# When the dots of the late rows are taken: fourth part instead of first, with their sends and one tile's transposes moved

## What is computed

```
s1, s2 = q . keys1, q . keys2            # 8 heads, 128 keys in each half
top 16 of each half, top 16 of their 256 sums -> eidx (of 16384 experts), gate = softmax
u = take(u_tab, eidx);  a = einsum('nhkd,nd->nhk', u, x)
w = gelu(a) * gate
y = einsum('nhk,nhkd->nd', w, take(v_tab, eidx))
```

## Time and profile before

| | us |
|---|---|
| median of 3 runs | 1452.32 (1451.91 to 1454.31) |
| profiled execution | 1451.67 |
| its span, first to last instruction | 1450.0 |
| PE busy | 1424.9 (98%) |
| PEld busy | 1266.6 (87%) |
| DVE busy | 1044.5 (72%) |
| POOL busy | 1017.7 (70%) |
| ACT busy | 608.9 (42%) |

### The profile page before, as it was taken

How to read it: one execution, slowest core, us unless ns; L and a number is a source line. 1 busy time by engine, 2 the same in 40 slices (tenths; PEclk the granted TensorE clock), 3 DMA queues, 4 the chain that set the end, 5 groups by cost and what they waited for, 6 DMA issues and landing times.

```text
span 1450.0 us, 24867 instructions
## 1 busy us (share of the span) xinstructions
PE 1424.9 (98%) x8029; PEld 1266.6 (87%) x8029; DVE 1044.5 (72%) x2204; ACT 608.9 (42%) x1018; POOL 1017.7 (70%) x631
## 2 busy tenths in 40 slices
PE   9999999999999999999999999999999999999996
PEld 5888788889999999999999999888888888888885
DVE  5466666688999989999987694875555555555587
ACT  5666741334333354444444443333333333333333
POOL 3332321335598877888877689898888888888886
PEclk9999999999999999999999999999999999999998
DMA  6212120424599889999999799999999999999981
GB/s 240 74 59 103 65 82 7 151 75 130 173 349 327 296 272 339 384 406 415 395 366 382 312 401 393 350 400 361 353 362 358 357 351 345 346 357 346 362 325 58
DMA packets 136907, 406.96 MB, mean 281 GB/s; under 512 B 13904, under 2 KB 56656, under 8 KB 134672
## 3 DMA queue, kind: packets, MB, share of 16 engines
q1 hardware_dynamic: 97088, 263.48, 50.3%
q0 software_dynamic: 39760, 142.76, 25.2%
HBM read 355.50 MB, written 50.14 MB: 280 GB/s over the span
## 4 chain that ended last, share of the span: by engine, by line
PE 85%; DVE 6%; ACT 2%; issue 2%; POOL 2%; DMA 2%; POOLq 0%; SPq 0%; ACTq 0%; DVEq 0%
PE banks L1824 14%; PE banks L1826 14%; PE banks L1825 14%; PE banks L1879 12%; PE banks L1881 12%; PE banks L1880 12%; PE banks L1941 2%; DMA raw<-u_t 1%; PE banks L2096 1%; PE banks L2097 1%; DVE rows L1363 1%; POOL lo L453 1%; PE banks L2033 1%; PE banks L1925 1%; DVE gate_hi L1593 1%
## 5 line engine op out<-in xcount | busy, mean ns | idle before, releaser
L453 POOL TENSOR_TENSOR lo<-raw,hi 128x1024 fp32r<-128x1024 f32 x292 | 706.8, 2422 | 349.5 <-ACT hi L447 330.2
L1824 PE MATMUL banks<-x1T_hi,hi 128*128 128x368 f32 (+3 forms) x1168 | 395.3, 338 | 0.7 <-POOL lo L453 0.4
L1825 PE MATMUL banks<-x1T_lo,hi 128*128 128x368 f32 (+3 forms) x1168 | 390.0, 334 | 0.0
L1826 PE MATMUL banks<-x1T_hi,lo 128*128 128x368 f32 (+3 forms) x1168 | 389.9, 334 | 0.0
L447 ACT ACTIVATE hi<-raw 128x1024 fp32r<-128x1024 f32 x292 | 307.1, 1052 | 30.2 <-DMA raw<-u_t 20.7
L1879 PE MATMUL banks<-hi,wgt_hi 128*128 128x512 f32 x750 | 291.8, 389 | 0.2 <-DVE wgt_lo L1701 0.2
L1881 PE MATMUL banks<-hi,wgt_lo 128*128 128x512 f32 x750 | 291.8, 389 | 0.0
L1880 PE MATMUL banks<-lo,wgt_hi 128*128 128x512 f32 x750 | 291.8, 389 | 0.0
L1701 DVE TENSOR_TENSOR wgt_lo<-wgt,wgt_hi 128x384 fp32r<-128x384 f32 x125 | 91.7, 734 | 193.0 <-ACT wgt_hi L1116 192.9
L1824 PEld LDWEIGHTS banks<-x1T_hi,hi 128*128 128x128 f32 x1168 | 219.3, 188 | 5.1 <-DVE x1T_lo L1335 0.6
L1826 PEld LDWEIGHTS banks<-x1T_hi,lo 128*128 128x128 f32 x1168 | 219.2, 188 | 4.4
(11 more groups left out here) (231 smaller groups left out, 1754.8 us busy)
## 6 DMA issues: line engine op xcount, KB each, us to landing
raw<-u_t SPq DMA_DIRECT2D x128, 512.0 KB, 5.6
raw<-v_tab SPq DMA_DIRECT2D x128, 512.0 KB, 6.8
g_scratch<-stage SPq DMA_DIRECT2D x12, 2048.0 KB, 11.0
gelu_scratch<-gelu SPq DMA_DIRECT2D x116, 192.0 KB, 7.5
ga<-gelu_scratch SPq DMA_DIRECT2D x29, 768.0 KB, 6.4
gg<-g_scratch SPq DMA_DIRECT2D x14, 1536.0 KB, 11.7
raw<-w SPq DMA_DIRECT2D x26, 512.0 KB, 3.4
raw<-w_pq SPq DMA_DIRECT2D x16, 512.0 KB, 3.5
```

Of the source, the lines that this page charges most:

```text
L453: eng.tensor_tensor(l[:, :], raw[:, c % RAW_SLOTS, :], h[:, :].bitcast(F32), ALU.subtract).then_inc(lo_ready, 1)
L1824: pe.matmul(o, h[:, s], hiT[:, k, tokens], start=(k == 0), stop=False)
L1825: pe.matmul(o, h[:, s], loT[:, k, tokens], start=False, stop=False)
L1826: ins = pe.matmul(o, l[:, s], hiT[:, k, tokens], start=False, stop=(k == KT - 1))
```

## The change

Eight edits, in the order of the program's time:

1. The six fill blocks of the last pair become twelve half blocks of three matmuls, at steps 2 to 7, 9 and 11 to 15.
2. x of the late tokens is no longer moved ahead of the search but in the first part (t = 7), into `sel[:, 0:2]`, free by then; `late_x` is no tensor of its own any more.
3. Four more gathers are asked for ahead of the first part (36 instead of 32); the gaps at tiles 25, 30 and 35 are filled, and tile 32 has two.
4. `turn_chosen` moves from tile 45 to tile 44, and `take_turned` stands ahead of tile 44's gelu.
5. In the first part GpSimd asks for 16 gathers (FIRST_MID_ROWS), all for the first 128 tokens, instead of 20, the first 16 of them for the late tokens.
6. The late numbers are moved at t = 2 of the first part (before: ahead of it, after tile 41), the late gates at t = 4 (before t = 3).
7. The late tokens' gathers and dots belong to the fourth part (LATE_O = 3). ScalarE puts their x into place near the end of the third part and takes it away near the end of the fourth; their weights are computed at the start of the fifth and moved at its t = 6 (before: after the second part).
8. So that the parts can differ, GpSimd's, VectorE's and some of ScalarE's and SyncE's loops over parts are written out.

```diff
-FIRST_ROWS_AT = (13, 13, 14, 15, 15, 16, 17, 17, 18, 19, 19, *range(20, 25), *range(26, 30),
-                 *range(31, 35), *range(36, 44))
+FIRST_ROWS_AT = (13, 13, 14, 15, 15, 16, 17, 17, 18, 19, 19, *range(20, 33), *range(32, 44))
 MID_ROWS = (2, 1, 1) * (MID_TILES // 3)
-LATE_ROWS = (0, 0, 0, 2, 3, 3, 2, 2, 2, 2, 2, 2)
+FIRST_MID_ROWS = (0, 0, 1, 1, 2, 2, 2, 2, 2, 2, 1, 1)
+LATE_O = 3
+R_LATE_AT = R_PRE + 2 * LATE_O
...
-        FILL_AT = {3: 0, 5: 1, 7: 2, 9: 3, 11: 4, 13: 5}
+        FILL_AT = (2, 3, 4, 5, 6, 7, 9, 11, 12, 13, 14, 15)
...
-            for g in range(SPREAD):
-                sp.dma_start(late_x[late_group(g), :], x1[LATE_AT:, TB - 1, :]).then_inc(late_x_moved, 16)
...
+            def move_x():
+                sp.wait_ge(sel_turned, 2)
+                for g in range(SPREAD):
+                    sp.dma_start(late_x[late_group(g), :], x1[LATE_AT:, TB - 1, :]).then_inc(late_x_moved, 16)
...
+            two_chunks(0, {2: move_numbers, 4: move_gates, 7: move_x})
+            with sp.Fori(1, LATE_O + 1) as o:
+                two_chunks(o)
+            two_chunks(LATE_O + 1, {6: move_weights})
...
+            for o in range(O_MID):
+                some_rows((R_PRE + 2 * o) * ROWS + AHEAD, 0, S_U + A_PRE + MID_TILES * o, 0,
+                          FIRST_MID_ROWS if o == 0 else MID_ROWS)
...
+            def late_dots_next():
+                act.wait_ge(late_x_moved, 16 * SPREAD)
+                act.wait_ge(row_used, R_LATE_AT * ROWS)
+                home(late_x)
...
-                        gelu_tile(tile % 4, 3 * o + (A_PRE // 4 + tile // 4))
                         if first and tile == 0:
                             take_turned()
-                        if first and tile == 1:
-                            act.wait_ge(late_x_moved, 16 * SPREAD)
-                            act.wait_ge(row_used, R_PRE * ROWS)
-                            home(late_x[:, :])
-                        if second and tile == 0:
-                            late_dots_done()
+                        gelu_tile(tile % 4, 3 * o + (A_PRE // 4 + tile // 4))
...
+                        if tile == MID_TILES - 3 and at_end is not None:
+                            at_end()
...
+            two_chunks(LATE_O - 1, at_end=late_dots_next)
+            two_chunks(LATE_O, at_end=late_dots_done)
...
+                    if tile == 0 and LATE_O <= o <= LATE_O + 1:
+                        dve.wait_ge(homes_ready, o - LATE_O + 3)
...
+                    if o == LATE_O + 1 and tile == 0:
+                        dve.wait_ge(late_gelu_ready, 1)
+                        dve.wait_ge(late_gates_moved, 16 * SPREAD)
+                        dve.tensor_tensor(late_weight, late_gelu, late_gates, ALU.mult).then_inc(late_weight_ready, 1)
...
                     if last and step in FILL_AT:
-                        mix_block(0, FILL_AT[step])
+                        mix_block(0, FILL_AT.index(step) // 2, FILL_AT.index(step) % 2)
...
-                    if first and tile == 1:
+                    if first and tile == 0:
                         turn_chosen(at)
```

More of the change, by code:

```diff
@@ L595, in move_weights, with two_chunks @@
                                  late_weight[late_group(g), :]).then_inc(late_weight_moved, 16)
-            def two_chunks(o, first=False):
+            def two_chunks(o, moves={}):
                 for t in range(MID_TILES):
                     store_and_load(t % 4, 3 * o + (A_PRE // 4 + t // 4))
-                    if first and t == 3:
-                        move_gates()
+                    if t in moves:
+                        moves[t]()
                     if t % (MID_TILES // 2) == MID_TILES // 2 - 1:
@@ L606, in two_chunks @@
                         sp.dma_start(g_dram[2 * o + half], stage[half][:, :, :]).then_inc(g_stored[half], 16)
-            with sp.Fori(0, A_PRE // 4 - 1) as it:
+            with sp.Fori(0, A_PRE // 4) as it:
                 for k in range(4):
                     store_and_load(k, it)
[L611 to L619, removed]
+            two_chunks(0, {2: move_numbers, 4: move_gates, 7: move_x})
+            with sp.Fori(1, LATE_O + 1) as o:
+                two_chunks(o)
+            two_chunks(LATE_O + 1, {6: move_weights})
+            for o in range(LATE_O + 2, O_MID):
                 two_chunks(o)
@@ L1101, in two_chunks @@
                                 stage_gates(half, o, group, first)
+                        if tile == MID_TILES - 3 and at_end is not None:
+                            at_end()
             two_chunks(0, first=True)
-            two_chunks(1, second=True)
-            with act.Fori(2, O_MID - 1) as o:
+            with act.Fori(1, LATE_O - 1) as o:
+                two_chunks(o)
+            two_chunks(LATE_O - 1, at_end=late_dots_next)
+            two_chunks(LATE_O, at_end=late_dots_done)
+            for o in range(LATE_O + 1, O_MID - 1):
                 two_chunks(o)
@@ L1367, in keep_dots @@
                 dve.wait_ge(row_used, ROWS * r + ROWS)
[L1369 to L1372, removed]
+                if r >= R_LATE_AT + R_LATE:
+                    kept_dots = dots[:, bass.ts(r - R_LATE, ROWS)]
+                elif r >= R_LATE_AT:
+                    kept_dots = late_dots[:, bass.ts(r - R_LATE_AT, ROWS)]
                 else:
@@ L1641, in _, with two_chunks @@
             one_hots(0, 0, True)
-            def two_chunks(o, first=False, second=False, last=False):
+            def two_chunks(o, last=False):
                 for tile in range(8):
@@ L1648, in two_chunks @@
                     elif not (last and tile == 7):
[L1649 to L1653, removed]
+                        one_hots(tile + 1, o, o == 0 and tile + 1 < HOT_SLOTS)
+                    if tile == 0 and LATE_O <= o <= LATE_O + 1:
+                        dve.wait_ge(homes_ready, o - LATE_O + 3)
                     for n in (2 * tile, 2 * tile + 1):
@@ L1657, in two_chunks @@
                             keep_dots(2 * o + (R_PRE + n // ROWS))
[L1659 to L1665, removed]
+                    if o == LATE_O + 1 and tile == 0:
+                        dve.wait_ge(late_gelu_ready, 1)
+                        dve.wait_ge(late_gates_moved, 16 * SPREAD)
+                        dve.tensor_tensor(late_weight, late_gelu, late_gates, ALU.mult).then_inc(late_weight_ready, 1)
+            for o in range(O_MID - 1):
                 two_chunks(o)
@@ L1966, in _, with mix_block @@
                 pair(j)
-            def mix_block(b, i):
+            def mix_block(b, i, half=None):
                 r = WOUT_ROWS[i]
-                if b == 0:
+                if b == 0 and half != 1:
                     if i == 0:
@@ L1980, in mix_block @@
                     pe.wait_ge(lo_ready, S_WOUT + i + 1)
-                return combine_block(b, S_WOUT + i, mixed(r), i == 0, i == KT - 1)
+                halves = range(2) if half is None else range(half, half + 1)
+                return combine_block(b, S_WOUT + i, mixed(r), i == 0, i == KT - 1, halves)
             pair(PAIRS - 1, last=True)
```

20 lines of the change are left out of this document (10 added, 10 removed).

## The result

| | before | changed |
|---|---|---|
| median, us | 1452.44 (1451.38 to 1454.31, 10 runs) | 1456.03 (1454.34 to 1458.03, 10 runs) |
| profiled execution, its span | 1451.67, 1450.0 | 1454.9, 1453.2 |

The ratio of the runs is 1.0026, 95% interval 1.0018 to 1.0034: the change costs 3.6 us. I had forecast 1446.7 us, in a range of 1444.9 to 1450.2.

A forecast was written before the change was run, and what follows sets the result against it. TensorE, busy 98% of the span, was taken as the bound, so only its gaps could be gained. 4.2 + 1.4 = 5.6 us off 1451.67 gave 1446.1 profiled, 1446.7 us as median; range 1444.9 to 1450.2.

The forecast's parts named there:

- The gaps that go: TensorE's three waits for gate_lo and the one for stage at 623.19 go: 4.2 us gained, bounds 0 and 4.9.
- The cast: VectorE's cast after selT, 2.95 us before, ends at 528.9 us with GpSimd's lo; under 1 us if right.
- Last pair: Half blocks in the last pair of heads bring the logits of steps 12 to 15 sooner: 1.4 us gained.
- my lower bound of -0.5: Last pair of heads: worst case -0.5 us, if the steps that lose half a block open a wait.
- Sends, cost 0: First part: sets of numbers, gates and x at t = 2, 4 and 7 don't add up on SyncE; cost 0.
- the landing of one store: First part: the store of tile 50's gelu lands at 578.7 us, 1.7 us late for tile 54's gelu, harmless to TensorE.
- Rival A: Slower: the three sets of sends pile up on SyncE and TensorE stands 9 us, 1455.7 us; chance 0.07.
- Gathers, cost 0: Four more gathers ahead of the parts, 16 instead of 20 in the first; GpSimd's reserve hides any hold; cost 0.
- Homes: ScalarE copies x after t = 9 of third and fourth part; VectorE waits up to 6 us each; cost 0, bounds 0 and 1.
- rival B: GpSimd is the new wait: tiles 53 and 54 wait about 1 us each for lo, 1448.7 us; chance 0.13.
- C: Only the turn pays: last pair gives nothing, one stall behind g_scratch (0.97) moves to the first part, 1449.1 us; chance 0.10.
- D: Nothing comes of it: store stalls and GpSimd's waits take back all four gaps, half blocks give 0.8 at most, 1451.5 us; chance 0.10.

The follow-up runs named there:

- x_small: The changed kernel with its eight sends of x cut to 64 columns each instead of 1024, the rest left out: 1450.62 us, ratio to before 0.9991.
- sends_later: The changed kernel with late numbers (t = 1) and x (t = 3) moved in the third part, gates (t = 3) in the fourth: 1448.34 us, ratio to before 0.9977.
- turn_only: The kernel before with one edit, turn_chosen at tile 44 and take_turned ahead of its gelu: 1450.27 us, ratio to before 0.9982.
- sends_later_fill_3: sends_later with the last pair's half fills at steps 3 to 9 and 11 to 15: 1447.65 us, ratio to before 0.9971.
- x_half: sends_later with x back at t = 7 of the first part, each send only 512 columns: 1450.53 us, ratio to before 0.9981.

## Why the prediction was wrong

- **The gaps that go: right.** Forecast -4.2, measured -3.23 (three waits for `gate_lo`) and -0.97 (`stage` at 623.19). The cast took 0.88 us and ended at 529.12, behind GpSimd's `lo` of 526.52 to 528.90 (forecast 528.9); the one-hots began at 530.35 (forecast 530.1).
- **Last pair: wrong in sign.** Forecast 1.4 gained, measured 0.32 lost. I moved fills by the reserve at the pair's end and didn't ask what the first half waits for; the loss lies within my lower bound of -0.5, but by luck: that bound was for steps that lose half a block, and the wait of 0.76 us stands at step 2, which gained one. What went at steps 14 and 15 came back as waits of 0.19 and 0.49 us for `probs_t`.
- **Sends, cost 0: this step failed.** It carried SyncE's time and the landing of one store (forecast 578.7, measured 580.4, harmless as I said), and stopped there. It never put x's own 512 KB into the ring, behind 2 MB that already make a store take 13 us, nor followed a later store than that of tile 50. That of tile 52, which tile 56's gelu needs, landed at 593.4 us. Measured: 4.86 us and 1.97 of slow clock, 6.8 us in all, for a term that I had put at 0.
- **Rival A** had the time nearly right, 1455.7 us, by luck, through another mechanism: SyncE late by 7 us. x_small holds SyncE as long and loses 3.3 us less. The sign of warning was in my own text: 12.6 us for 192 KB.
- **Gathers, cost 0: failed too.** I counted 20 less 4 as relief for the DMA engines and let GpSimd's reserve hide the rest. I didn't ask what GpSimd's order does to SyncE: in the changed kernel the 2 MB store goes out at 566.91 us, and even without sends at 566.09 (sends_later), while in turn_only, with the same turn and the old gathers, it goes out at 561.94. Three gathers moved bring it to 560.56 and take 3.6 us off the stall.
- **Homes: right.** VectorE waited 6.88 us twice, and no wait of TensorE came of it. GpSimd's waits of rival B did not appear; C and D named a stall behind the store, but with 1 us, or no more than the gaps were worth.
- Left out altogether: the clock after a stall, and the 0.6 us at 926 us, if they belong to the change.

With the sends out of the first part and the first fill a step later, the change gives the 4.2 us that the working had for the gaps, and 0.35 of the 1.4 for the last pair: 1451.67 less both is 1447.1, and sends_later_fill_3's profiled execution took 1446.95 us.

## What to carry over

Where a wait is for a landed store, follow the bytes in the ring, not the issuing queue's time: list what is issued between a large store and the moment the ring is empty again, and add every byte of it to the landing of each later one. Put such bytes ahead of the store or a part later; that alone was worth 6 us here. Follow each buffer of a ring of four, not only the first that meets the large store: the wait that showed was two tiles behind the one that I had followed. And ask what holds the engines whose work the queue waits for, since that sets when the large store goes out.

## What was not expected of the hardware

Copies from SBUF to SBUF of 64 KB, rows of 4 KB, took the DMA engines' rate from 420 to 305 GB/s at the same busy share. A stall of 4.70 us left the granted clock at 0.50 for 4.3 us more. The length of the stall alone doesn't tell: after 2.51 us in turn_only it stayed at 1.00, after 2.00 us in x_half it fell, as this window of x_half shows:

```profile
594.00:596.00 2.00, 2.00 (x12) 2.00 (x10) 2.00 (x2) 1.93 (x3) 1.85 (x2) 0.50 1.06 436
```
